# An MLP in seven-product form: the split halves of the weight sums are no longer kept in DRAM; each of the three blocks splits all seven weight forms again

## The reference, cut to what matters

```
h  = x + concatenate([attn_out, lru_out]) @ w_out
hn = rmsnorm(h, norm_ffn_g)
y  = h + square(relu(hn @ w_up)) @ w_down      # w_up 1024x4096, w_down 4096x1024
out = rmsnorm(y, final_norm_g)
```

## Time and profile before

| | |
|---|---|
| three runs | 2146.77, 2148.1, 2150.18 us |
| the profiled execution's own time | 2146.69 us |
| its span | 2144.9 us |
| phase 1 / block 0 / block 1 / block 2 / last tiles | 0 to 760 / 760 to 1212 / 1212 to 1663 / 1663 to 2121 / to 2144.9 us |
| TensorE weight loads, busy | 88% of the span |
| VectorE, ScalarE, busy | 71%, 47% |
| moved by DMA | 500.91 MB |

### The profile page before, as it was taken

One profiled execution on the slowest core, in us unless ns is written; L12 is line 12 of the kernel. 1 busy time (PEld: TensorE's weight loads), 2 busy tenths in 40 slices (PEclk: granted clock), 3 DMA queues, 4 the chain that ended last, 5 costly groups with the idle time before them and its releaser, 6 DMA issues.

```text
span 2144.9 us, 34224 instructions
## 1 busy us (share of the span) xinstructions
PE 1983.0 (92%) x11669; PEld 1878.0 (88%) x11669; DVE 1527.9 (71%) x2183; ACT 1011.2 (47%) x1967; POOL 430.8 (20%) x393
## 2 busy tenths in 40 slices
PE   6789889988987989999999989999999899999994
PEld 6778778777776779999999889999999799999994
DVE  7767867777678788878887966667767766666663
ACT  5555454544544555555555534433335533333331
POOL 3536656555567100100000001000000000000000
PEclk9889999999999999999999999999999999999997
DMA  6767676776755599989999887768878777777761
GB/s 178 226 174 225 176 238 197 209 234 192 214 188 161 167 300 316 317 287 298 345 326 299 290 270 243 230 205 267 272 220 269 239 213 217 216 217 216 216 211 63
DMA packets 396538, 500.91 MB, mean 234 GB/s; under 512 B 27498, under 2 KB 301450, under 8 KB 396394
## 3 DMA queue, kind: packets, MB, share of 16 engines
q1 hardware_dynamic: 394698, 493.38, 74.3%
q0 software_dynamic: 1696, 5.67, 0.8%
HBM read 375.36 MB, written 123.68 MB: 233 GB/s over the span
## 4 chain that ended last, share of the span: by engine, by line
PE 67%; DVE 10%; issue 8%; POOL 7%; DMA 3%; ACT 3%; SPq 1%; POOLq 0%; DVEq 0%; ACTq 0%
PE results L2056 19%; PE tail L2056 14%; PE scores_a L2056 14%; PE results L1840 10%; PE aux L2056 8%; DVE w_lo L1356 2%; PE aux L1960 1%; DVE hn_lo L1497 1%; POOL prob L929 1%; POOL xrow L898 1%; DMA out<-yout 1%; POOL xrow L902 1%; POOL xrow L900 1%; POOL third L900 1%; POOL sumsq L867 1%
## 5 line engine op out<-in xcount | busy, mean ns | idle before, releaser
L1035 ACT ACTIVATE w_hi<-w_raw 128x512 fp32r<-128x512 f32 (+1 forms) x360 | 240.8, 690 | 380.8 <-PE results L2056 160.5
L1507 DVE TENSOR_TENSOR w_lo<-w_raw,w_hi 128x512 fp32r<-128x512 f32 (+1 forms) x360 | 275.7, 779 | 49.0 <-ACT w_hi L1035 48.8
L1840 PE MATMUL results<-xg_hi,w_hi 128*128 128x448 f32 (+1 forms) x560 | 216.1, 386 | 27.6 <-DVE w_lo L1356 21.6
L1840 PE MATMUL results<-xg_lo,w_hi 128*128 128x448 f32 (+1 forms) x560 | 203.5, 363 | 0.0
L1840 PE MATMUL results<-xg_hi,w_lo 128*128 128x448 f32 (+1 forms) x560 | 203.0, 363 | 0.0
L2056 PE MATMUL results<-hn_hi,w_hi 128*128 128x348 f32 x576 | 187.4, 325 | 10.9 <-DVE x L1753 5.0
L971 ACT ACTIVATE w_hi<-raw 128x1024 fp32r<-128x1024 f32 x110 | 116.4, 1058 | 160.3 <-PE results L1840 156.8
L1356 DVE TENSOR_TENSOR w_lo<-raw,w_hi 128x1024 fp32r<-128x1024 f32 x110 | 155.4, 1413 | 49.5 <-ACT w_hi L971 49.5
L2056 PE MATMUL results<-hn_hi,w_lo 128*128 128x348 f32 x576 | 185.8, 323 | 0.0
L2056 PE MATMUL results<-hn_lo,w_hi 128*128 128x348 f32 x576 | 185.6, 322 | 0.0
L2056 PE MATMUL scores_a<-hn_hi,w_hi 128*128 128x348 f32 x480 | 155.8, 325 | 2.2 <-DVE x L1753 1.8
(11 more groups left out here) (274 smaller groups left out, 5665.7 us busy)
## 6 DMA issues: line engine op xcount, KB each, us to landing
w_lo<-s_scratch SPq DMA_DIRECT2D x128, 512.0 KB, 4.5
w_hi<-s_scratch SPq DMA_DIRECT2D x256, 256.0 KB, 3.5
w_raw<-in_w_up SPq DMA_DIRECT2D x144, 256.0 KB, 4.5
w_raw<-in_w_down SPq DMA_DIRECT2D x144, 256.0 KB, 4.3
raw<-in_w_in SPq DMA_DIRECT2D x70, 512.0 KB, 5.1
w_raw<-s_raw SPq DMA_DIRECT2D x64, 512.0 KB, 5.5
s_scratch<-w_lo SPq DMA_DIRECT2D x64, 512.0 KB, 5.9
s_scratch<-w_hi SPq DMA_DIRECT2D x128, 256.0 KB, 6.0
```

The lines of the kernel that those rows point to most:

```text
L1035: nc.scalar.activation(ring(w2_hi, u, ks[0], len(ks)), raw_slots(u, ks[0], len(ks)), ACT.Copy)\
L1507: nc.vector.tensor_tensor(w2_lo[u.s][:, PHYS[ks[0]]:PHYS[ks[0]] + len(ks), :], raw_slots(u, ks[0], len(ks)), ring(w2_hi.bitcast(F32), u, k ...
L1840: last = nc.tensor.matmul(out, wt, x(kx), start=(start and i == 0 and part == 0), stop=(stop and i == len(ks) - 1 and part == 2))
```

## The change

The DRAM tensor `s_scratch` is gone, with its stores (`store_s`), the loads of high parts (`load_high`) and the semaphores `s_out`, `hi_out` and `hi_in`. `load_part` loads the whole sums out of `s_raw` in every block. `weights_high` and `weights_low` no longer skip the sums in blocks 1 and 2, and a product waits for `wlo_done` alone.

```diff
     def split(self, k):
-        if self.first:
-            return 7 * self.g + k + 1
-        return 7 * UN + 3 * (self.g - UN) + (0, 3, 6).index(k) + 1
-
-    def times(self):
-        return (self.g - UN) // 2 + 1
+        return 7 * self.g + k + 1
...
-        s_dram = nc.dram_tensor("s_scratch", (UN, P, 8, 512), F32, kind="Internal").ap()
...
             def load_part(g, part):
                 u = Unit(g)
-                half = part // 2
-                if part in (1, 3) and 2 <= g < UN + 2:
-                    sp.wait_ge(s_out[u.s][half], 16 * ((g - 2) // 2 + 1))
-                if part in (1, 3) and u.first:
-                    sp.dma_start(raw_slots(u, 1 + 3 * half, 2), s_raw[P * (u.i + 4):P * (u.i + 5), 2 * half:2 * half + 2, :])\
-                      .then_inc(w2_in[u.s][part], 16)
-                elif part in (1, 3):
-                    sp.wait_ge(s_out[u.s][half], 16 * (u.i // 2 + 1))
-                    sp.dma_start(low_slots(u, 1 + 3 * half, 2), s_dram[u.i][:, 2 * half:2 * half + 2, :])\
+                if part in (1, 3):
+                    k, half = (1, 0) if part == 1 else (4, 1)
+                    sp.dma_start(raw_slots(u, k, 2), s_raw[P * (u.i + 4):P * (u.i + 5), 2 * half:2 * half + 2, :])\
                       .then_inc(w2_in[u.s][part], 16)
...
-            def load_high(g, k):
...
-                sp.dma_start(ring(w2_hi.bitcast(F32), u, k), s_dram[u.i][:, 4 + j:5 + j, :]).then_inc(hi_in[u.s][j], 16)
-
-            def store_s(g, half):
...
-                sp.dma_start(s_dram[u.i][:, 2 * half:2 * half + 2, :], low_slots(u, k, 2)).then_inc(s_out[u.s][half], 16)
-                for j in (2 * half, 2 * half + 1):
-                    sp.dma_start(s_dram[u.i][:, 4 + j:5 + j, :], ring(w2_hi.bitcast(F32), u, SUMS[j])).then_inc(hi_out[u.s][j], 16)
...
-                if UN <= g + 1 < G and k + 1 in SUMS:
-                    load_high(g + 1, k + 1)
...
-                if g == 0 and k == 0:
-                    store_s(0, 0)
-                if u.first and k == 2:
-                    store_s(g, 1)
-                if g + 1 < UN and k == 4:
-                    store_s(g + 1, 0)
...
             def weights_high(g, k):
-                if g == G or k in SUMS and g >= UN:
+                if g == G:
                     return
...
-                            if old < UN and ok in SUMS:
-                                act.wait_ge(hi_out[old % 2][SUMS.index(ok)], 16 * (old // 2 + 1))
...
             def weights_low(g, k):
-                if g == G or k in SUMS and g >= UN:
+                if g == G:
                     return
...
             def weights_ready(u, k):
-                if u.first or k in (0, 3, 6):
-                    pe.wait_ge(wlo_done, u.split(k))
-                else:
-                    part = u.sum_part(k)
-                    pe.wait_ge(w2_in[u.s][part], 16 * (u.g // 2 + 1))
-                    pe.wait_ge(hi_in[u.s][SUMS.index(k)], 16 * u.times())
+                pe.wait_ge(wlo_done, u.split(k))
```

More of the change, by code:

```diff
@@ L372, in build_program @@
         w2_in = [[sem(f"w2_in{s}{p}") for p in range(5)] for s in range(2)]
-        s_out = [[sem(f"s_out{s}{p}") for p in range(2)] for s in range(2)]
-        hi_out = [[sem(f"hi_out{s}{p}") for p in range(4)] for s in range(2)]
-        hi_in = [[sem(f"hi_in{s}{p}") for p in range(4)] for s in range(2)]
         sums_in, sums_out = [sem(f"sums_in{j}") for j in range(3)], [sem(f"sums_out{j}") for j in range(3)]
@@ L584, in load_part @@
                     sp.dma_start(dst, quarter(u, k)).then_inc(w2_in[u.s][part], 16)
-            def load_high(g, k):
-                u, j = Unit(g), SUMS.index(k)
-                old, ok = divmod(7 * g + k - 8, 7)
-                sp.wait_ge(prod_done, Unit(old).product(ok))
-                if old < UN and ok in SUMS:
-                    sp.wait_ge(hi_out[old % 2][SUMS.index(ok)], 16 * (old // 2 + 1))
-                sp.wait_ge(hi_out[u.s][j], 16 * (u.i // 2 + 1))
-                sp.dma_start(ring(w2_hi.bitcast(F32), u, k), s_dram[u.i][:, 4 + j:5 + j, :]).then_inc(hi_in[u.s][j], 16)
-            def store_s(g, half):
-                u, k = Unit(g), 1 + 3 * half
-                sp.wait_ge(wlo_done, u.split(k + 1))
-                sp.dma_start(s_dram[u.i][:, 2 * half:2 * half + 2, :], low_slots(u, k, 2)).then_inc(s_out[u.s][half], 16)
-                for j in (2 * half, 2 * half + 1):
-                    sp.dma_start(s_dram[u.i][:, 4 + j:5 + j, :], ring(w2_hi.bitcast(F32), u, SUMS[j])).then_inc(hi_out[u.s][j], 16)
             def load_sums(blk, v):
@@ L840, in _ @@
             sp.wait_ge(h_stored, 64 + 32 * NB1)
-            for s in range(2):
-                for half in range(2):
-                    sp.wait_ge(s_out[s][half], 16 * UN // 2)
-                for j in range(4):
-                    sp.wait_ge(hi_out[s][j], 16 * UN // 2)
             for h in range(2):
```

## The result

The kernel after is slower by a quarter of a per cent.

| | before | after |
|---|---|---|
| median (lowest to highest) | 2148.11 us (2145.13 to 2153.03) | 2155.26 us (2146.16 to 2159.28) |
| ratio, 95% interval | | 1.0025 [1.0013, 1.0036] |
| profiled execution, its span | 2146.69, 2144.9 us | 2155.35, 2153.4 us |
| start of phase 2 | 759.98 us | 761.45 us |
| phase 2 without the last tiles | 1350.8 us | 1357.5 us |

A forecast was written before the change was run, and what follows sets the result against it. TensorE was taken to bound the MLP, so its waits count. Terms -5.4 - 3.6 - 2.0 + 6.5 + 9.4 + 1.0 = +5.9 us gave 2154.0 us on the median of 2148.1 (1.4 over the profiled 2146.7), range 2145 to 2162.

The forecast's parts named there:

- unit 0: First unit of block 0: without the store, 3.8 us of waiting and 1.6 us of low clock go; gain 5.4 us.
- unit 31: Before the first change of blocks: the wait for the next block's late input goes, half of it clock; gain 3.6 us.
- stores of output tiles: At block changes: 0.5 us off each of ScalarE's four waits, as DMA engines are less busy; gain 2 us.
- steady r = 2 units: 13 units of blocks 1 and 2 go from 13.35 to 13.86 us, VectorE's added split overrunning its cover; +6.5 us.
- changes of blocks: Two stretches where TensorE follows VectorE: added splits cost 4.7 us each, output tiles moving rigidly with VectorE; +9.4 us.
- units 45 and 46: Around a reciprocal in block 1: a split behind it, before an add TensorE waits for, costs +1.0 us for both.
- 0.98 us of cover: Unit 38: the add ends 0.98 us before product 4 starts; a 1.23 us split ahead overruns by 0.25.
- remaining wait of 1.3 us: In unit 0: TensorE's 5.03 us wait for VectorE's add was to shrink to some 1.3 us without the store.
- A: Rival, faster: VectorE has room, steady units lose nothing, block changes cost 1.8 instead of 4.7; -7.4 us, 2141, chance 0.09.
- B: Rival, no change: gaps at block changes absorb half the splits, stores land sooner; +0.9 us, 2149, chance 0.22.
- the sign that the prediction set for it: Sign for B: units 32 to 34 together take less than 3 us more than before.
- C: Rival, slower: waits in units 0 and 31 are not relieved, only 1.8 of 11.0 won; +15 us, 2163, chance 0.14.

The follow-up runs named there:

- e1: Kernel before without its stores to s_scratch and the waits for them, blocks 1 and 2 loading as many bytes from s_raw as stand-ins; 2136.12 us.
- e5: Kernel after with VectorE's split of forms 4 and 5 in r = 2 units cut in two, form 5's behind product 2's add; 2145.89 us, ratio 0.9985.
- e9: Kernel before with first store early, each block's last two units' sums not kept, forms 4 and 5 split apart, output-tile buffers swapped; 2126.25 us, ratio 0.9909.
- e2: Kernel after with VectorE's split of forms 4 and 5 in r = 2 units of blocks 1 and 2 cut to 8 columns; 2147.63 us.
- e4: Kernel after with VectorE's splits of the four sums in units 32, 33, 64 and 65 cut to 8 columns; 2148.29 us.
- e8: Kernel after with output-tile buffers swapped: even tiles in hid_y, odd ones in yout, so the last leaves hid_y; 2142.01 us, ratio 0.9976.
- e10: Kernel after with ScalarE's copy of forms 4 and 5 (r = 2, blocks 1 and 2) and GpSimd's norm adds cut to 8 columns; 2153.21 us.

## Why the prediction was right

The interval of the ratio, put on 2148.1 us, is 2150.9 to 2155.8 and holds the forecast of 2154.0. The terms came out as follows. The price of the stores is read from e1 against the kernel before, that of the splits from the kernel after against e1:

| term | forecast | measured |
|---|---|---|
| unit 0 | -5.4 | -5.2 |
| unit 31 | -3.6 | -3.6 |
| stores of output tiles | -2.0 | -1.3 in e1 (32 to 34: -0.8, 64 to 66: -0.4), within the spread |
| steady r = 2 units | +6.5 | +6.9 |
| changes of blocks | +9.4 | +8.4 (31 to 34: +4.5, 63 to 66: +3.8) |
| units 45 and 46 | +1.0 | +1.2 |
| sum, with 0.3 in the rest | +5.9 | +6.8 |

The rows on the output tiles' stores and on the changes of blocks can't be told apart, since e1 keeps the loads of high parts: what their going gives is in the +8.4. Together they are +7.4 forecast and +7.1 measured.

- *Steady units, r = 2.* Right in mechanism and size. The 0.98 us of cover, compared with the 1.23 us of the split, gave the answer before any run, and e5 shows the other side of the same threshold: 0.69 us ahead of the adds fits. One of the 13 units (86, 14.21 us) lost 0.4 more: VectorE stands idle for 0.37 us just before its split there, and the trace names no one that it waits for.
- *Unit 0: right in both terms, wrong about where the clock goes.* The 3.8 us of waiting came: VectorE's split starts 13.89 us into the unit instead of 17.71, and the product behind it 15.68 instead of 19.51. The 1.6 us of clock came as 1.4: that last product of the unit took 3.37 us behind the long wait, at a mean clock of 0.55, and takes 1.99 at 1.00. Windows of it, before and after:

```profile
779.49:782.86 3.37, 3.37 (x13) 3.37 (x14) 3.18 (x6) 1.65 (x5) 0.00 (x0) 0.55 1.04 405
```
```profile
777.13:779.12 1.99, 1.99 (x13) 1.99 (x13) 1.96 (x4) 1.38 (x3) 0.00 (x0) 1.00 0.68 208
```

  Wrong was to take the fall of the clock to be gone. It falls earlier in the unit, whose mean is 0.90 after and was 0.93 before, but it costs nothing there: in e9 the unit has a mean of 1.00 and takes the same 17.67 us, because VectorE is busy for 17.28 of them. Without the store unit 0 is bound by VectorE. Wrong too was the remaining wait of 1.3 us. It is 0.28, since TensorE at its lower clock comes to it late; in e9, at the higher one, it is 1.18:

```profile
777.13 0.40 PE L2007 MATMUL results<-hn_hi,w_hi 128*128 128x348 f32 x1 [0.28 <-DVE x L1704]
```
```profile
775.45 0.40 PE L2060 MATMUL results<-hn_hi,w_hi 128*128 128x348 f32 x1 [1.18 <-DVE x L1756]
```

  A mean clock times a duration is a cost only where TensorE is the bound.
- *Units 45 and 46.* +0.60 and +0.64. In e2, without the split of forms 4 and 5 in unit 46, that unit gives back 0.80 and unit 45 nothing; what costs unit 45 its 0.60 no run isolates.
- *Changes of blocks.* 4.7 each, and 4.5 and 3.8 measured, but only in part as argued. Units 31 and 32 pay for the splits (e4: -1.06 and -1.24 without them). That the storing and reuse of the output tiles "move rigidly with VectorE" is not borne out: the tiles' chain ends in a store, unit 33 took 19.72 to 22.33 us behind the same work of VectorE, and e4's gain in 31 and 32 was partly lost again in front of it. e8 shows that this chain is worth 10 us, more than the change itself. Since unit 33 or 65 alone can differ by 2.6 us from one execution to the next, the two prices are known no better than that, and that their sum came so near is in part luck.
- *Stores of output tiles: the mechanism is there, at other stores than the term had it.* I took 0.5 us off each of four landings, because the DMA engines would be less busy. Six tiles are stored at a change of blocks. At the third, in `yout`, the engines were less busy; at the sixth, in `hid_y`, they were not. The third, for which ScalarE waits in unit 33, from issue to landing, before and after:

```profile
1240.62:1246.58 5.96, 5.96 (x44) 5.94 (x44) 2.61 (x5) 1.49 (x3) 1.05 (x2) 1.00 0.98 335
```
```profile
1237.82:1241.36 3.54, 3.54 (x26) 3.54 (x26) 3.50 (x7) 1.48 (x3) 1.04 (x2) 1.00 0.54 146
```

  With the DMA engines' share at 0.54 instead of 0.98 it takes 2.42 us less, and by just that ScalarE's wait for it is shorter, 1.31 us instead of 3.73:

```profile
1241.44 1.03 ACT L1185 ACTIVATE yout<-aux 116x1024 f32<-116x1024 f32 x1 [1.31 <-DMA out<-yout]
```

  The same store at the second change of blocks went from 4.64 us at a share of 0.97 to 3.53 at 0.52. The sixth store went the other way, 4.09 to 5.67 us (share 0.94 and 0.90) and 5.94 to 6.33 (0.95 and 0.99), and the wait for it from 5.01 to 6.59 and from 6.85 to 7.24. All waits of ScalarE for these stores together fell from 18.7 to 16.4 us; how much of that TensorE got, no run shows. The median landing at the first change of blocks hides it, 5.7 us and then 5.5:

```profile
DMA to landing us min/median/max: 3.5/5.5/7.2
```

  e1 can't show it, since with the loads of high parts in place the share stays at 0.96 and that store at 6.11 us. ScalarE waits for it as before:

```profile
1236.58 1.03 ACT L1215 ACTIVATE yout<-aux 116x1024 f32<-116x1024 f32 x1 [3.88 <-DMA out<-yout]
```

  The Trainium skill's rule (DMA: Bandwidth & Descriptors, Latency and other measured facts) that a lighter load on HBM makes a DMA's fixed cost smaller agrees in direction with the two stores whose share fell. The estimate of 7 us made from it does not come out: ScalarE's waits fell by 2.2 us in all, and at the sixth store the engines' load was no lighter.
- *The rivals.* A (VectorE has room) falls by e2: taking one instruction away in each unit gave back 6.9 us. The Trainium skill's rule (Perfetto Trace Analysis, Identifying the Most-Contended Engine) names the engine with the highest occupancy, here TensorE with its weight loads at 98%, and this trace agrees. What A read into it, that work added to VectorE at 81% is free, this trace contradicts. B (the changes absorb the splits) falls in its sum: with units 31 and 63 and the stores, B had +2.4 for the changes of blocks and +7.1 was measured. But the sign that the prediction set for it, units 32 to 34 less than 3 us up, did come, with +2.6 (and +2.3 for 64 to 66). The sign was badly placed: 1.1 us of the splits' price falls in units 31 and 63, outside its window, and against e1 units 32 to 34 are up by 3.4. What e4 showed as given back in units 33 and 34 would be B's mechanism. C (waits not relieved) falls by units 0 and 31.

## What to carry to other kernels

When work is added to an engine with idle time, don't ask how busy it is, but which instruction stands ahead of the one that the bound engine waits for, and how many tenths of a microsecond lie between them; cutting that instruction in two and moving one half behind the add gave back 5.7 of 6.9 us. When a side product (here a stored split) makes a wait, first move its transfer in the queue: the change paid 17 us of splits to be rid of 10 us of waits, of which a store moved up in its queue and two units left out of the keeping removed some 6.5. Judge a change of a few microseconds by unit, since one profiled span beside another was moved by more than that by a phase that nobody touched.

## What the runs showed of the hardware

- A VectorE subtraction with both inputs in SBUF waits for GpSimd's add to end. One of 128x348 (0.51 us alone) took 2.04 us when it started 0.24 us after GpSimd's add of 128x696, also all in SBUF, and ended 0.38 us after that add; one of 128x1024 took 1.83 instead of 1.23. In e2, too, two splits of 128x512 beside such an add took 2.19 us. With GpSimd's add cut to 8 columns the first two were back at 0.52 and 1.23 (e10). In the kernel after a like add (1313.66, 1.71 us) ran beside VectorE's adds to `hcur`, which read one input from PSUM; they took 0.87 to 0.88 as always. The Trainium skill says the same (SBUF — State Buffer, Who interferes with whom): a VectorE instruction with two SBUF inputs contends with a GpSimd instruction that reads SBUF, and the one that was issued later blocks until the other is through. The trace agrees for the case in which GpSimd's is first. Such a stall is why a shift of a microsecond, in a kernel that changes nothing else, can cost 1.5 us in one unit.
- Unit 0 takes 17.67 us at a mean granted clock of 0.90 (the kernel after) and of 1.00. Its window in e9:

```profile
759.76:777.43 17.67, 14.19 (x84) 13.41 (x85) 17.28 (x19) 8.96 (x15) 0.00 (x0) 1.00 0.97 338
```

- At the changes of blocks waits and the lower clock come together: TensorE idles for 5.3 and 5.7 us in units 34 and 66 of the kernel after, at a mean clock of 0.84; in e8 it idles for 2.8 and 1.2, at 0.91 and 1.00.
- The same store of an output tile took 5.96 us from issue to landing with the DMA engines at 0.98 (before) and 3.54 at 0.54 (after); at the second change of blocks it took 4.64 at 0.97 and 3.53 at 0.52.
